# The last chunk of the last product in three parts (256, 128, 128 tokens) in place of two of 256

## The reference

```
h2 = rms_norm(x, norm_mlp[l])
x = x + jnp.square(jax.nn.relu(h2 @ w_up[l])) @ w_down[l]
return rms_norm(x, norm_final)
```

## Time and profile before

| | us |
|---|---|
| median of three runs | 1150.37 |
| the profiled execution, its time | 1150.57 |
| the profiled execution, its span | 1148.8 |
| TensorE busy in the span | 1129.4 |
| VectorE (DVE) busy | 638.4 |
| ScalarE (ACT) busy | 518.6 |
| GpSimd (POOL) busy | 160.8 |

### The profile page before, as it was taken

The page is one execution under the profiler, slowest core; times in us unless marked ns, Lnnn a source line. Parts: engine busy times, 40 slices in busy tenths (PEclk is TensorE's granted clock), DMA queues, the critical chain, the costliest instruction groups (busy, mean ns, idle before and its releaser), DMA issues.

```text
span 1148.8 us, 14370 instructions
## 1 busy us (share of the span) xinstructions
PE 1129.4 (98%) x5342; PEld 890.7 (78%) x5342; DVE 638.4 (56%) x1083; ACT 518.6 (45%) x904; POOL 160.8 (14%) x198
## 2 busy tenths in 40 slices
PE   9999899999999999999999999999999999999997
PEld 6787677887666778867777878888888888888886
DVE  7787887854667775455544545555544233444232
ACT  6657666544666554244444533335433112443231
POOL 2012112310223312022211200011000000000021
PEclk9999999999999999999999999999999999999999
DMA  6322222332111123211223223223223233233312
GB/s 226 111 74 92 92 73 93 111 110 74 56 56 56 56 74 107 96 56 56 92 75 111 74 65 101 91 93 110 92 92 110 92 100 102 92 92 102 100 55 74
DMA packets 30806, 102.82 MB, mean 90 GB/s; under 512 B 3344, under 2 KB 5648, under 8 KB 30736
## 3 DMA queue, kind: packets, MB, share of 16 engines
q1 hardware_dynamic: 30304, 101.37, 27.2%
q10 hardware_dynamic: 432, 0.52, 0.1%
HBM read 99.78 MB, written 2.10 MB: 89 GB/s over the span
## 4 chain that ended last, share of the span: by engine, by line
PE 83%; DVE 9%; ACT 5%; issue 2%; DMA 0%; SPq 0%; DVEq 0%; ACTq 0%
PE ps L693 25%; PE ps L695 24%; PE ps L694 24%; PE ps L817 3%; DVE xs L1253 2%; PE ps L829 2%; PE ps L860 2%; DVE wl L1178 2%; ACT Pt L1057 1%; PE ps L854 1%; PE ps L765 1%; ACT xs L939 1%; ACT wh L892 1%; DVE cc L1285 1%; DVE sg L1269 1%
## 5 line engine op out<-in xcount | busy, mean ns | idle before, releaser
L693 PE MATMUL ps<-xgh,wh 128*128 128x512 f32 x848 | 345.3, 407 | 6.0 <-DVE wl L1178 5.6
L695 PE MATMUL ps<-xgh,wl 128*128 128x512 f32 x848 | 332.2, 392 | 0.0
L694 PE MATMUL ps<-xgl,wh 128*128 128x512 f32 x848 | 331.8, 391 | 0.0
L1178 DVE TENSOR_TENSOR wl<-raw,wh 128x1024 fp32r<-128x1024 f32 x180 | 229.5, 1277 | 133.1 <-ACT wh L892 131.1
L892 ACT ACTIVATE wh<-raw 128x1024 fp32r<-128x1024 f32 x180 | 188.6, 1049 | 130.5 <-PE ps L695 130.1
L693 PEld LDWEIGHTS ps<-xgh,wh 128*128 128x128 f32 x848 | 159.9, 189 | 57.6 <-issue 26.9
L695 PEld LDWEIGHTS ps<-xgh,wl 128*128 128x128 f32 x848 | 159.8, 188 | 34.3
L694 PEld LDWEIGHTS ps<-xgl,wh 128*128 128x128 f32 x848 | 160.1, 189 | 33.6 <-issue 3.1
L1638 POOL TENSOR_SCALAR Pt<-Pt,stat 128x256 f32<-128x256 f32 (+2 forms) x128 | 76.5, 610 | 293.0 <-DVE stat L1416 217.8
L1057 ACT ACTIVATE Pt<-Pt,stat 128x256 f32<-128x256 f32 (+2 forms) x128 | 64.5, 504 | 98.9 <-DVE stat L1388 38.1
L693 PE MATMUL ps<-fh,wh 128*128 128x512 f32 x240 | 93.4, 389 | 0.0
(11 more groups left out here) (219 smaller groups left out, 1574.1 us busy)
## 6 DMA issues: line engine op xcount, KB each, us to landing
raw<-wst SPq DMA_DIRECT2D x180, 512.0 KB, 3.4
bst<-nbias SPq DMA_DIRECT2D x8, 256.0 KB, 3.4
xt<-xT SPq DMA_DIRECT2D x3, 512.0 KB, 7.7
outT<-ot SPq DMA_DIRECT2D x2, 384.0 KB, 2.5
outT<-ot SPq DMA_DIRECT2D x6, 128.0 KB, 2.0
raw<-wst SPq DMA_DIRECT2D x2, 256.0 KB, 4.4
cstt<-cst SPq DMA_DIRECT2D x1, 512.0 KB, 5.8
xt<-xT ACTq DMA_DIRECT2D x1, 256.0 KB, 3.7
```

The source lines that it names most:

```text
L693: e.matmul(o, high, a, start=(k == 0), stop=False)
L694: e.matmul(o, high, b, start=False, stop=False)
L695: e.matmul(o, low, a, start=False, stop=stop).then_inc(tile_done, 1)
L1178: e.tensor_tensor(wl_t[:, u % NHL, :], raw_t[:, u % NRAW, :], f32(wh_t[:, u % NHL, :]), ALU.subtract).then_inc(lo_done, 1)
```

## The change

The last chunk is written in three parts: 256, 128 and 128 tokens. All that was done for each of two halves is now done for each of three parts: 48 matmuls (of 128 columns for the last two parts), an add, a square, a product with ones (and one with `ssq`), Ln, two Exp, six DVE rows and two GpSimd rows. Each part has two banks of its own; Exp writes back to the part's norm bank. The rows of every part go out three at a time from SyncE, GpSimd's two rows in one transfer, for the last part from ACT. An output row of 128 tokens is 512 bytes a partition. The last part's transfers were eight (six from SyncE and two from ACT) and are three.

```diff
-        halves = [slice(0, 256), slice(256, 512)]
-        last_acc = [bank[(ch.bank["dn", 1, 7] + i) % 7][:, 0:256] for i in (0, 2)]
-        last_bank = [bank[n][:, 0:256] for n in (NB, (ch.bank["dn", 1, 7] + 1) % 7)]
+        parts = [slice(0, 256), slice(256, 384), slice(384, 512)]
+        part_end = [LAST + c.stop / 32 for c in parts]
+        FINAL = len(parts) - 1
+        after_last = (ch.bank["dn", 1, 7] + n for n in (0, 2, 3, 1, 4))
+        last_acc = [bank[next(after_last) % 7][:, 0:c.stop - c.start] for c in parts]
+        last_bank = [bank[NB][:, 0:256]] + [bank[next(after_last) % 7][:, 0:c.stop - c.start] for c in parts[1:]]
...
-                c = halves[1]
-                for j in range(NP, KD):
-                    q.wait_ge(fin_done, KD - NP + j - NP + 1)
-                    e.dma_start(out[:, j, c], ot[:, j, c]).then_inc(out_done, 16)
-                q.wait_ge(out_done, 16 * (3 + KD))
+                for i, c in enumerate(parts):
+                    for j in range(NP, KD, 3):
+                        q.wait_ge(fin_done, (KD - NP) * i + j - NP + 3)
+                        e.dma_start(out[:, j:j + 3, c], ot[:, j:j + 3, c]).then_inc(out_done, 16)
+                    if i < FINAL:
+                        q.wait_ge(fin2_done, NP * (i + 1))
+                        e.dma_start(out[:, 0:NP, c], ot[:, 0:NP, c]).then_inc(out_done, 16)
+                q.wait_ge(out_done, 16 * 3 * len(parts))
...
-                for i in range(2):
-                    o, c = last_acc[i], halves[i]
+                for i, c in enumerate(parts):
+                    o = last_acc[i]
                     for k in range(16):
-                        yield LAST + 8.0 * i + 0.5 * k
+                        yield LAST + c.start / 32 + k * (c.stop - c.start) / 512
                         wait_bank(q, ("dn", 1, 7))
-                        q.wait_ge(ev_done, ev_no(("dn", 1, 2)))
+                        q.wait_ge(ev_done, ev_no(("dn", 1, 3)))
...
-                q.wait_ge(ev_done, ev_no(("dn", 1, 1)))
-                for i in range(2):
-                    e.matmul(last_bank[i], C_("ones"), ssq[:, 256 * i:256 * i + 256], start=True, stop=False)
-                for i in range(2):
-                    yield (LAST + 10.2, 4000.0)[i]
+                q.wait_ge(ev_done, ev_no(("dn", 1, 4)))
+                for o, c in zip(last_bank, parts):
+                    e.matmul(o, C_("ones"), ssq[:, c], start=True, stop=False)
+                for i, c in enumerate(parts):
+                    yield part_end[i] + 2.2 if i < FINAL else 4000.0
...
-                for i in range(2):
-                    for j in range(NP, KD):
-                        yield (LAST + 11.5, 4020.0)[i]
+                for i, c in enumerate(parts):
+                    for j in range(NP, KD):
+                        yield part_end[i] + 3.5 + (0.8 if j > NP + 2 else 0.0)
```

More of the change, by code:

```diff
@@ L295, in build @@
         out_done = sem("out_done")
-        warm_done, tile_done, first_half, nb_done, n4_done = (
-            sem(n) for n in ("warm_done", "tile_done", "first_half", "nb_done", "n4_done"))
+        warm_done, tile_done, part_done, nb_done, n4_done = (
+            sem(n) for n in ("warm_done", "tile_done", "part_done", "nb_done", "n4_done"))
         hsum_done, perm_done = sem("hsum_done"), sem("perm_done")
@@ L310, in build @@
             sem(n) for n in ("rstd8_done", "y2h_done", "gt_done", "mh_done", "fsq_done", "fh_done", "xf_done"))
-        lo_done, xl_done, kvl_done, odd_done, drv_done, ev_done, half_done = (
-            sem(n) for n in ("lo_done", "xl_done", "kvl_done", "odd_done", "drv_done", "ev_done", "half_done"))
+        lo_done, xl_done, kvl_done, odd_done, drv_done, ev_done, added = (
+            sem(n) for n in ("lo_done", "xl_done", "kvl_done", "odd_done", "drv_done", "ev_done", "added"))
         conv_done = [sem(f"conv_done{i}") for i in range(2)]
@@ L709, in gemm @@
                         done = e.matmul(o, low, a[:, c], start=False, stop=(k == 15))
-                        if i:
+                        if i == FINAL:
                             done.then_inc(tile_done, 1)
                         elif k == 15:
-                            done.then_inc(first_half, 1)
+                            done.then_inc(part_done, 1)
             def norm(s, tick):
@@ L738, in last_norm @@
                 q.wait_ge(rstd_done, 4)
-                q.wait_ge(ev_done, ev_no(("dn", 1, 1)))
-                for i in range(2):
-                    e.matmul(last_bank[i], C_("ones"), ssq[:, 256 * i:256 * i + 256], start=True, stop=False)
-                for i in range(2):
-                    yield (LAST + 10.2, 4000.0)[i]
+                q.wait_ge(ev_done, ev_no(("dn", 1, 4)))
[3 more added lines that the diff above has]
+                    yield part_end[i] + 2.2 if i < FINAL else 4000.0
                     q.wait_ge(sq_done, 49 + i)
-                    e.matmul(last_bank[i], C_("ones"), sq[0][:, halves[i]], start=False, stop=True).then_inc(n4_done, 1)
+                    e.matmul(last_bank[i], C_("ones"), sq[0][:, c], start=False, stop=True).then_inc(n4_done, 1)
             def warm_up():
@@ L924, in last_root @@
             def last_root():
-                for i, c in enumerate(halves):
-                    yield (LAST + 10.8, 4012.0)[i]
+                for i, c in enumerate(parts):
+                    yield part_end[i] + 2.8
                     q.wait_ge(n4_done, i + 1)
@@ L931, in last_root @@
                     q.wait_ge(ln_done, 5 + i)
-                    e.activation(bank[NB][:, c], sq[1][:, c], ACT.Exp, scale=-0.5).then_inc(rstd_done, 1)
+                    e.activation(last_bank[i], sq[1][:, c], ACT.Exp, scale=-0.5).then_inc(rstd_done, 1)
                     e.activation(rstd[:, c], sq[1][:, c], ACT.Exp, scale=-0.5).then_inc(lr_done, 1)
@@ L1128, in last_squares @@
                 for j in range(KD):
-                    yield ev_at["dn", 1, j] + 0.5 if j < KD - 1 else LAST + 8.5
+                    yield ev_at["dn", 1, j] + 0.5 if j < KD - 1 else part_end[0] + 0.5
                     q.wait_ge(sum_done, 27 + j if j < 2 else 28 + j - 1)
                     if j == KD - 1:
-                        for i, c in enumerate(halves):
-                            if i:
-                                yield LAST + 17.5
+                        for i, c in enumerate(parts):
+                            yield part_end[i] + 0.5
+                            if i == FINAL:
                                 q.wait_ge(ev_done, ev_no(("dn", 1, j)))
                             else:
-                                q.wait_ge(half_done, 1)
+                                q.wait_ge(added, i + 1)
                             e.activation(sq[0][:, c], xt[:, j, c], ACT.Square).then_inc(sq_done, 1)
@@ L1146, in stores @@
                 yield 5000
[L1147 to L1150, removed]
+                c = parts[FINAL]
+                q.wait_ge(fin2_done, NP * len(parts))
+                e.dma_start(out[:, 0:NP, c], ot[:, 0:NP, c]).then_inc(out_done, 16)
             lanes = [load_x0(), weights_high(), first_high(), first_squares(), exp_lambda(), head_squares(), head_roots(), outs(), eighth(), gates_c(), merged_high(), last_squares(), last_root(), stores()]
@@ L1549, in downs @@
                 if hf and j == KD - 1:
[L1550 to L1557, removed]
+                    for i, c in enumerate(parts):
+                        yield part_end[i] + 0.2
+                        if i < FINAL:
+                            q.wait_ge(part_done, i + 1)
+                        else:
+                            q.wait_ge(tile_done, end["dn", 1, j] + 1)
+                        e.tensor_tensor(xt[:, j, c], last_acc[i], xt[:, j, c], ALU.add).then_inc(
+                            *((added, 1) if i < FINAL else (ev_done, 1)))
                     return
@@ L1564, in finals @@
             def finals():
-                for i, c in enumerate(halves):
+                for i, c in enumerate(parts):
                     for j in range(NP, KD):
-                        yield (LAST + 11.5, 4020.0)[i]
+                        yield part_end[i] + 3.5 + (0.8 if j > NP + 2 else 0.0)
                         q.wait_ge(rstd_done, 5 + i)
                         q.wait_ge(par_in, 16)
-                        e.scalar_tensor_tensor(ot[:, j, c], xt[:, j, c], P_("fin_g", j), bank[NB][:, c], ALU.mult, ALU.mult).then_inc(fin_done, 1)
+                        e.scalar_tensor_tensor(ot[:, j, c], xt[:, j, c], P_("fin_g", j), last_bank[i], ALU.mult, ALU.mult).then_inc(fin_done, 1)
             lanes = [weights_low(), first_low(), first_sums(), derive(), heads(), head_norm(), key_copies(), value(), key_a(),
@@ L1640, in finals @@
             def finals():
-                for i, c in enumerate(halves):
+                for i, c in enumerate(parts):
                     for j in range(NP):
-                        yield (LAST + 11.5, 4020.0)[i]
```

(1 more changed line is left out.)

## The result

| | before | after |
|---|---|---|
| median, us (6 runs each) | 1150.01 | 1153.39 |
| lowest and highest, us | 1149.12 to 1151.38 | 1152.81 to 1155.07 |
| the profiled execution: time, span | 1150.57, 1148.8 | 1155.07, 1153.3 |

The ratio is 1.0029, with a 95% interval of 1.0019 to 1.0039: 3.4 us slower, where 3.4 was forecast.

A forecast was written before the change was run, and what follows sets the result against it. TensorE, busy 98% of the span, was taken to bound the kernel, with a tail behind it. +4.80 + 0.21 - 0.05 - 0.67 - 0.85 = +3.44 us, forecast 1153.8 us, range 1151.4 to 1155.4.

The forecast's parts named there:

- The stream: TensorE, last chunk's second half: 96 steps of 0.11 us replace 48 of 0.12, plus a norm product; ends 4.96 us later.
- load and hand-over add up: Rival for TensorE's 128-column matmuls: hand-over comes on top of the load, 0.12 us a step, 1154.8 us; chance 0.2.
- columns bind: Rival for TensorE's 128-column matmuls: loads overlap each other, 0.067 us a step, -0.4 us, 1149.9 us; chance 0.08.
- steps in between: Rival for TensorE's 128-column matmuls: loads share some work, 0.081 us a step, +0.7 us, 1151.0 us; chance 0.1.
- The chain of the last part: Last part's add, square, norm product, Ln and Exp after TensorE's stream: 128 columns fewer save 0.67 us.
- The bytes: Last part's output transfers: 512-byte packets at 27 ns, last byte 3.5 us after DVE's first product, not 4.35; 0.85 us saved.
- slow short packets: Rival for the output transfers: 512-byte packets still take 43 ns each, with steps of 0.11 us, 1154.8 us; chance 0.1.
- The waits behind the moved adds: Work queued on DVE and ACT around the moved adds: costs 0; with 0.067 us steps the last add is 0.25 late.
- The total: Whole kernel: stream's growth less what the last part's chain and bytes save, +3.44 us.

## Why the prediction was right

- **The stream.** The step that the forecast hung on, 0.11 read from two loads on an idle array, is 0.1114 in the stream. That it is the load's columns is shown from both sides: 64 columns of load give 0.060, 64 rows leave 0.11, 64 streamed columns leave 0.11. It is not the output that a matmul writes either (64 tokens against 64 channels, above). The term was 0.21 too small: 0.13 because of 96 x 0.0014, 0.05 because the last matmul ended no sooner (in a load-bound stream its record is 0.275 and not 0.23 long); 0.03 I can't place.
- **The rival "load and hand-over add up"** (0.12) is out: what a step of 256 columns has beyond its columns, 0.0134, hides under a load, at least where the load binds. The run with 240 tokens says so too; from its second matmul after the norm's product to its last (timeline) are 31 steps in 3.46 us, 0.1116 each, where columns and hand-over would make 0.1134:

```profile
1136.30 0.27 PE L708 MATMUL ps<-fl,wh 128*128 128x240 f32 x1
...
1139.76 0.28 PE L709 MATMUL ps<-fh,wl 128*128 128x240 f32 x1
```

- **The rivals "columns bind" and "steps in between"** are out by the same step. The 81 ns a matmul that the Trainium skill gives (page "TensorE: Matmul & The Clock Gate", section "Back-to-back issue gap") does not hold for this type: 111 ns. Its section "LDWEIGHTS (loading the stationary operand)" gives the load's time by its columns alone, whatever the rows; the runs with 64 columns and with 64 rows agree.
- **The chain of the last part** gave back 0.67, as worked out from the slopes between 512 and 256 columns.
- **The bytes.** Forecast 0.85, found 0.92. Packets of 512 bytes took 24 ns where I had taken 27; that was a choice between 21 and 43 with no row for it, so that this term came out so near is in part luck. The rival of slow short packets is out. The transfers before did not run "at a steady 385 GB/s" from the first byte on, as the prediction reads them: two slices show the gap named above, worth some 0.2 us; the sum goes from the measured last byte and is not touched.
- **The waits behind the moved adds** cost nothing in the change: the second part's three products end at 1146.37, the add comes at 1147.10. In the run with steps of 0.060 they did cost the 0.2 that was forecast for such steps.
- **The total.** By the pieces +3.58 for a forecast of +3.44: the stream's 0.21 too little and the bytes' 0.07 too little saved partly cancel.

The clock is what the prediction did not ask about. It found it at 1.00 and took it for given; the change kept it, but the runs with 64 rows and with 64-token parts lost some 9 us to it, and the one with 96 rows 4.

## What to carry to other kernels

Where each matmul has its own load of 128 columns, a float32 product here pays at least 0.11 us a matmul, so cutting tokens into parts costs the steps nearly nothing down to 240 columns a part, where the step is already 0.1116, and below that 0.11 less the columns' time for each load. (0.111 less 0.0134 at 2.4 GHz would put the floor at 235 columns, but the run with 240 was at it already; so it begins between 240 and 256.) Each further part also puts its norm's product into the stream, 0.42 us with 256 tokens here and 0.22 with 128. Work out the loads first, then what the tail gives back (12 ns a token here, 1.6 us for 128 tokens). Read a stream by the distance of its starts, since it is "100% busy" whether columns or loads bind. Grouped or single transfers are a question of what ends last, bytes or issues, and by the profiles the answer changed sign between 128 and 256 tokens.

## What the runs showed of the hardware that I had not expected

TensorE's clock fell to half in streams without a single pause. It fell after 2 to 3 us of matmuls with 64 streamed columns in steps of 0.11 (two executions of two), after 3 us of matmuls of 128 columns on 64 rows, after 7 us on 96 rows, and not in 22 us of 128 columns on 128 rows, nor in 6 us of 128 columns in steps of 0.060 with 64 columns of weights. All of these stretches read 100% busy. The step's length alone does not sort the cases, since matmuls in steps of 0.11 stand among those that kept the clock and those that lost it, and neither does the number of rows, since the clock fell with full rows too. What does is not shown.

Nor does the moment of a fall say much. The change and the run with single rows give TensorE the same matmuls to the end. The stream's last one ends at 1147.06 in the change and at 1145.13 in the run, the norm's product at 1148.27 and 1146.35. The stretches in which the clock then fell, first the change's and then those of the run with single rows:

```profile
1150.00:1151.00 1.00, 0.00 (x0) 0.00 (x0) 0.66 (x3) 0.00 (x0) 0.16 (x1) 1.00 0.25 71
1151.00:1152.00 1.00, 0.00 (x0) 0.00 (x0) 0.00 (x0) 0.00 (x0) 0.00 (x0) 0.56 1.14 341
...
1147.00:1148.00 1.00, 0.00 (x0) 0.00 (x0) 0.90 (x4) 0.29 (x2) 0.63 (x2) 0.62 0.91 276
1148.00:1149.00 1.00, 0.00 (x0) 0.00 (x0) 0.74 (x3) 0.00 (x0) 0.23 (x1) 0.50 0.58 172
```

It fell 4 us after the last matmul of the stream in one and 2 us after it in the other. In the run of 384 and 128 tokens it was a microsecond, in the kernel before 4.7 (granted 1.00 to 1145, 0.84 in the next microsecond). So the differences of a few microseconds between one execution with 64 rows and one with 96 are not a measure of anything yet.
